# Stick-breaking attention: work by PSUM bank, suffix sums prepared on VectorE, values of two heads in turn, and the causal mask added by VectorE

## What is computed

```
z = einsum('bhqd,bhkd->bhqk', qb, kb) * scale
mask = s_pos < t_pos
log_keep = where(mask, log_sigmoid(-z), 0)
suffix = cumsum(log_keep, reverse) - log_keep
wts = where(mask, exp(log_sigmoid(z) + suffix), 0)
out = einsum('bhqk,bhkd->bhqd', wts, vb)
```

## Time and profile before

| | |
|---|---|
| median of 3 executions | 1835.47 us (1831.92 to 1836.16) |
| span of the profiled execution, first to last instruction | 1824.3 us |
| PE busy | 1705.0 us, 93% of the span |
| DVE, ACT busy | 647.0 us, 443.7 us |
| attention, first score to the end of the last values | 202.1 to 286.3 us, 84.2 us |

### The profile page before, as it was taken

The page is one execution under the profiler, slowest core; times in us unless marked ns, Lnnn a source line. Parts: engine busy times, 40 slices in busy tenths (PEclk is TensorE's granted clock), DMA queues, the critical chain, the costliest instruction groups (busy, mean ns, idle before and its releaser), DMA issues.

```text
span 1824.3 us, 21872 instructions
## 1 busy us (share of the span) xinstructions
PE 1705.0 (93%) x8774; PEld 885.3 (49%) x8774; DVE 647.0 (35%) x1210; ACT 443.7 (24%) x775; POOL 170.2 (9%) x172
## 2 busy tenths in 40 slices
PE   7999999889999999999699998999799999999983
PEld 3455564545445555455355548975433333333331
DVE  3379111242223122221269947542522221222213
ACT  2233552214312122111258512331100000000001
POOL 0000000011111111110000023100111111111110
PEclk9999999989999999999899999999799999999997
DMA  9274611389999999999480091044799999999994
GB/s 367 93 257 160 213 70 47 133 321 407 392 401 411 407 400 406 407 411 413 174 322 1 5 143 47 1 162 194 277 392 403 406 409 407 406 421 408 417 414 175
DMA packets 94220, 515.26 MB, mean 282 GB/s; under 512 B 22429, under 2 KB 28157, under 8 KB 69544
## 3 DMA queue, kind: packets, MB, share of 16 engines
q1 hardware_dynamic: 82920, 496.46, 70.0%
q0 software_dynamic: 11200, 17.39, 2.9%
HBM read 506.09 MB, written 27.05 MB: 292 GB/s over the span
## 4 chain that ended last, share of the span: by engine, by line
PE 70%; DMA 15%; issue 7%; DVE 5%; SPq 2%; ACT 1%; DVEq 0%; POOLq 0%
PE bank L852 22%; PE bank L868 10%; PE bank L454 8%; PE bank L462 8%; DMA ring<-in_w_up 7%; DMA ring<-in_w_down 4%; PE bank L809 3%; PE bank L839 3%; PE bank L730 2%; PE bank L879 2%; PE bank L520 2%; PE bank L685 2%; PE bank L447 1%; DVE arena L2549 1%; DMA ring<-diag 1%
## 5 line engine op out<-in xcount | busy, mean ns | idle before, releaser
L854 PE MATMUL bank<-ring,arena 128*64 128x512 f32 x928 | 418.7, 605 | 0.0
L852 PE MATMUL bank<-ring,arena 128*64 128x512 f32 x752 | 339.1, 604 | 9.4 <-DMA ring<-in_w_up 6.8
L868 PE MATMUL bank<-ring,arena 128*64 128x512 f32 x544 | 247.9, 598 | 2.6 <-DMA ring<-in_w_down 2.6
L870 PE MATMUL bank<-ring,arena 128*64 128x512 f32 x544 | 247.9, 598 | 0.0
L2448 DVE TENSOR_TENSOR arena<-arena,bank 64x512 f32<-64x512 f32 x70 | 48.3, 690 | 560.5 <-ACT arena L1763 560.5
L454 PE MATMUL bank<-arena,ring 128*128 128x512 f32 x560 | 244.6, 593 | 0.0
L852 PEld LDWEIGHTS bank<-ring,arena 128*64 128x64 f32 x752 | 100.7, 139 | 208.5 <-issue 202.4
L852 PE MATMUL bank<-arena 128*64 128x512 f32 x368 | 166.1, 605 | 9.3 <-DMA ring<-in_w_up 5.0
L1429 POOL DMA_INDIRECT arena<-xnd,smalli x70 | 67.6, 966 | 1074.4 <-PE bank L839 536.0
L454 PEld LDWEIGHTS bank<-arena,ring 128*128 128x128 f32 x560 | 105.2, 190 | 127.2 <-issue 127.2
L1763 ACT ACTIVATE arena<-bank 64x512 f32<-64x512 f32 x70 | 41.2, 588 | 512.1 <-PE bank L854 512.1
(11 more groups left out here) (439 smaller groups left out, 1999.2 us busy)
## 6 DMA issues: line engine op xcount, KB each, us to landing
ring<-in_w_down SPq DMA_DIRECT2D x62, 2048.0 KB, 33.2
ring<-in_w_up SPq DMA_DIRECT2D x54, 2048.0 KB, 16.9
ring<-in_w_gate SPq DMA_DIRECT2D x45, 2048.0 KB, 17.4
arena<-in_w_gate SPq DMA_DIRECT2D x19, 2048.0 KB, 25.2
ring<-in_w_mod SPq DMA_DIRECT2D x12, 2048.0 KB, 8.0
ring<-in_w_in SPq DMA_DIRECT2D x10, 2048.0 KB, 15.7
arena<-in_w_up SPq DMA_DIRECT2D x10, 2048.0 KB, 29.8
ring<-in_w_out SPq DMA_DIRECT2D x4, 2048.0 KB
```

The costliest lines, as they stand in the source:

```text
L852: pe.matmul(GU[0:CAP, :], x, wg_[:, c, :], start=(c == 0), stop=(c == KD - 1), skip_group_check=True)
L854: mm = pe.matmul(GU[CAP:2 * CAP, :], x, wu_[:, c, :], start=(c == 0), stop=(c == KD - 1), skip_group_check=True)
L868: pe.matmul(Y[0:CAP, :], x, wd_[:, c, 0:512], start=(c == 0), stop=(c == 3), skip_group_check=True)
L870: mm = pe.matmul(Y[CAP:2 * CAP, :], x, wd_[:, c, 512:1024], start=(c == 0), stop=(c == 3), skip_group_check=True)
```

## The change

Five edits, all in the attention:

1. By bank. `PIECES` orders a head's work: the third bank (256 columns), the second (chunks 1 and 3, 512 columns), the first (512 columns). `z_ready`, `ln_ready`, `sp_raw`, `arg_ready` and `w_raw` are counted three to a head, and each step waits only for its own bank. Exp and Ln of the softplus become three instructions each, interleaved.
2. Sums of later chunks. After two of its three instructions `scored` adds the columns of later chunks up on DVE into `below` (three additions of 128x128), and `decays` multiplies `nones` with these sums: nine products and 2048 columns in place of ten and 2560.
3. `values(p)` works on two heads: their products alternate between the lower and the upper 64 output partitions. It stands once for each pair, after `scores` of the pair's second successor.
4. Mask. The four identity products of `scores` go; a new `masked(h)` on DVE adds `far` to the four diagonal blocks in PSUM.
5. Order. PE runs `decays(2p)`, `scores(2p+2)`, `decays(2p+1)`, `scores(2p+3)`, `values(p)`; DVE runs `scored(h)`, `masked(h+1)`.

```diff
+        PIECES = ((2, 256, (2,)), (1, 512, (1, 3)), (0, 512, (0,)))
+        below = [area(5, 3072 + 384 * i, 384) for i in range(2)]
...
             def scores(h):
-                for c in (0, 1, 3, 2):
-                    pe.matmul(zpart(z, c), ...)
-                for c in range(4):
-                    mm = pe.matmul(zpart(z, c)[:, 0:P], M["ident"], far, start=False, stop=True,
-                                   skip_group_check=True)
+                for i, (bank, width, held) in enumerate(PIECES):
+                    if h >= 2:
+                        pe.wait_ge(S("w_raw"), 3 * (h - 2) + i + 1)
+                    for c in held:
+                        mm = pe.matmul(zpart(z, c), ...)
+                    mm.then_inc(S("z_ready"), 1)
...
             def decays(h):
-                for c in range(4):
-                    for c2 in range(c, 4):
-                        mm = pe.matmul(zpart(z, c)[:, P * (c2 - c):], M["nge"] if c2 == c else M["nones"],
-                                       kpart(spb[h % 2], c2), start=False, stop=(c2 == 3),
-                                       skip_group_check=True)
-                mm.then_inc(S("arg_ready"), 1)
+                pe.wait_ge(S("sp_raw"), 3 * h + 2)
+                less(2, 2, 4, M["nge"], kpart(sp, 2), False)
+                less(2, 3, 4, M["nones"], kpart(sp, 3), True).then_inc(S("arg_ready"), 1)
+                less(3, 3, 4, M["nge"], kpart(sp, 3), True)
+                less(1, 1, 4, M["nge"], kpart(sp, 1), False)
+                less(1, 2, 3, M["nones"], kpart(sp, 2)[:, 0:P], True)
+                pe.wait_ge(S("below"), 3 * h + 1)
+                less(1, 3, 4, M["nones"], bl[:, 2 * P:3 * P], True).then_inc(S("arg_ready"), 1)
+                pe.wait_ge(S("sp_raw"), 3 * h + 3)
+                less(0, 0, 4, M["nge"], kpart(sp, 0), False)
+                less(0, 1, 2, M["nones"], kpart(sp, 1)[:, 0:P], True)
+                pe.wait_ge(S("below"), 3 * h + 3)
+                less(0, 2, 4, M["nones"], bl[:, 0:2 * P], True).then_inc(S("arg_ready"), 1)
...
+            def values(p):
+                pe.wait_ge(S("w_raw"), 3 * (2 * p + 2))
                 for c in range(4):
+                    for i in range(2):
+                        h, r = 2 * p + i, HD * i
+                        mm = pe.matmul(o[r:r + HD, P * c:T], vtok[:, c, HD * h:HD * h + HD], kpart(wb[i], c),
+                                       start=(c == 0), stop=(c == 3), skip_group_check=True)
...
-            for h in range(NH):
-                decays(h)
-                if h:
-                    values(h - 1)
-                if h + 2 < NH:
-                    scores(h + 2)
-            values(NH - 1)
+            for p in range(NH // 2):
+                for h in (2 * p, 2 * p + 1):
+                    decays(h)
+                    if h + 2 < NH:
+                        scores(h + 2)
+                values(p)
...
             def softplus(h):
-                for b, w in ((0, 512), (1, 512), (2, 256)):
-                    last = A(lnb[:, 512 * b:512 * b + w], z[b][:, 0:w], ACT.Abs)
-                chain(last)
-                chain(A(lnb, lnb, ACT.Exp, scale=-1.0))
-                A(lnb, lnb, ACT.Ln, bias=one).then_inc(S("ln_ready"), 1)
+                absolute(0)
+                exponential(0)
+                absolute(1)
+                logarithm(0)
+                exponential(1)
+                absolute(2)
+                logarithm(1)
+                exponential(2)
+                logarithm(2)
...
+            def masked(h):
+                z = zbanks[h % 2]
+                for i, (bank, width, held) in enumerate(PIECES):
+                    dve.wait_ge(S("z_ready"), 3 * h + i + 1)
+                    for c in held:
+                        o = zpart(z, c)[:, 0:P]
+                        ins = TTo(o, o, far, ALU.add)
+                    ins.then_inc(S("z_masked"), 1)
...
             def scored(h):
+                    if i == 1:
+                        dve.wait_ge(S("sp_raw"), 3 * h + 2)
+                        TTo(bl[:, 2 * P:3 * P], kpart(sp, 2)[:, P:2 * P], kpart(sp, 3), ALU.add).then_inc(S("below"), 1)
+                        TTo(bl[:, 0:P], kpart(sp, 1)[:, P:2 * P], kpart(sp, 2)[:, 0:P], ALU.add).then_inc(S("below"), 1)
+                        dve.wait_ge(S("below"), 3 * h + 1)
+                        TTo(bl[:, P:2 * P], kpart(sp, 1)[:, 2 * P:3 * P], bl[:, 2 * P:3 * P], ALU.add)\
+                            .then_inc(S("below"), 1)
...
             for h in range(1, NH):
                 scored(h)
+                if h + 1 < NH:
+                    masked(h + 1)
```

More of the change, by code:

```diff
@@ L735, in values @@
[L735 to L741, removed]
+                for i, (bank, width, held) in enumerate(PIECES):
+                    if h >= 2:
+                        pe.wait_ge(S("w_raw"), 3 * (h - 2) + i + 1)
+                    for c in held:
+                        mm = pe.matmul(zpart(z, c), qk[r:r + HD, 4 + h // 2, P * c:P * c + P],
+                                       qk[r:r + HD, h // 2, P * c:T], start=(c != 3), stop=False,
+                                       skip_group_check=True)
+                    mm.then_inc(S("z_ready"), 1)
@@ new lines, in decays, with less @@
+            def decays(h):
+                z, sp, bl = zbanks[h % 2], spb[h % 2], below[h % 2]
+                def less(c, q0, q1, mat, src, last):
+                    return pe.matmul(zpart(z, c)[:, P * (q0 - c):P * (q1 - c)], mat, src, start=False, stop=last,
+                                     skip_group_check=True)
+                pe.wait_ge(S("sp_raw"), 3 * h + 2)
[11 more added lines that the diff above has]
+                less(0, 2, 4, M["nones"], bl[:, 0:2 * P], True).then_inc(S("arg_ready"), 1)
@@ L1308, in _ @@
             load_e(0, 3)
-            sp.wait_ge(S("z_ready"), NH)
+            sp.wait_ge(S("z_ready"), 3 * NH)
             sp.dma_start(x_tok, a["x"].rearrange("(t p) d -> p t d", p=P)).then_inc(S("x_again"), 16)
@@ L1698, in softplus, with part, marked, absolute @@
                 z = zbanks[h % 2]
-                act.wait_ge(S("z_ready"), h + 1)
-                if h:
-                    act.wait_ge(S("sp_raw"), 3 * h)
-                for b, w in ((0, 512), (1, 512), (2, 256)):
-                    last = A(lnb[:, 512 * b:512 * b + w], z[b][:, 0:w], ACT.Abs)
-                chain(last)
-                chain(A(lnb, lnb, ACT.Exp, scale=-1.0))
-                A(lnb, lnb, ACT.Ln, bias=one).then_inc(S("ln_ready"), 1)
+                def part(i):
+                    bank, width, _ = PIECES[i]
+                    return lnb[:, 512 * bank:512 * bank + width], z[bank][:, 0:width]
+                at = {}
+                def marked(ins, name):
+                    chained[0] += 1
+                    ins.then_inc(S("act_chain"), 1)
+                    at[name] = chained[0]
+                def absolute(i):
+                    act.wait_ge(S("z_masked"), 3 * h + i + 1)
+                    if h:
+                        act.wait_ge(S("sp_raw"), 3 * (h - 1) + i + 1)
+                    marked(A(part(i)[0], part(i)[1], ACT.Abs), f"abs{i}")
+                def exponential(i):
+                    act.wait_ge(S("act_chain"), at[f"abs{i}"])
+                    marked(A(part(i)[0], part(i)[0], ACT.Exp, scale=-1.0), f"exp{i}")
+                def logarithm(i):
+                    act.wait_ge(S("act_chain"), at[f"exp{i}"])
+                    A(part(i)[0], part(i)[0], ACT.Ln, bias=one).then_inc(S("ln_ready"), 1)
+                absolute(0)
[7 more added lines that the diff above has]
+                logarithm(2)
             def squared(p):
@@ L1718, in _ @@
                 z = zbanks[h % 2]
-                act.wait_ge(S("arg_ready"), h + 1)
                 if h >= 2:
-                    act.wait_ge(S("o_ready"), h - 1)
-                for b, w in ((0, 512), (1, 512), (2, 256)):
-                    A(wb[h % 2][:, 512 * b:512 * b + w], z[b][:, 0:w], ACT.Exp).then_inc(S("w_raw"), 1)
+                    act.wait_ge(S("o_ready"), h // 2)
+                for i, (bank, width, _) in enumerate(PIECES):
+                    act.wait_ge(S("arg_ready"), 3 * h + i + 1)
+                    A(wb[h % 2][:, 512 * bank:512 * bank + width], z[bank][:, 0:width], ACT.Exp).then_inc(S("w_raw"), 1)
                 if h + 2 < NH:
```

31 lines of the change are left out of this document (14 added, 17 removed).

## The result

The changed kernel takes 1809.38 us (median of 4 executions, 1806.15 to 1811.33), the kernel before 1835.37 beside it: a ratio of 0.9859, 95% interval 0.9844 to 0.9874.

The account below looks back on a forecast made before the run. PE was taken to set the attention's pace, and later stages to shift with it: 20.9 us saved less 2 for waits is 18.9, so 1835.5 - 18.9 = 1816.6, say 1817 us; range 1811 to 1825.5.

Parts of the forecast that it names:

- The work on PE: PE in the attention, a pair of heads: decays 7.0, scores 4.70, values 2.30, together 14.0 us, now 20.16.
- The walk: Attention followed joint by joint from the first score at 202.11: project at 265.4 before the allowance, 20.9 us sooner.
- The allowance: Semaphore waits within each engine's row, bounded by nothing and 4.0 us; half taken, 2 us, giving a gain of 18.9.
- The clock (D): Rival: PE's clock halves after the new 2.8 us stand at the start, losing 1.9 us; folded into the 62% forecast case.
- The loop (B): Rival: the loop through ACT and DVE is longer than summed; gain 11 to 16, 1820 to 1824.5 us; 22%.
- the values (C): Rival: values of two heads don't share the PE array, 4.6 us a pair; gain 9.7, 1826 us; 5%.
- slower (E): Rival: the loop takes 11.2 us, binding both heads of a pair; 7.4 us more than before, 1843; 4%.
- given back (F): Rival: the MoE waits for something not moving with PE, up to all lost; 1830 to 1841; 4% with smaller losses.
- The step that failed: From project to the end: each us by which project starts sooner is a us of the end; nothing else changes.
- The 11.2 us: Median's excess over the profiled span of 1824.3 us, taken as untouched by the change.
- or a better clock behind: Part of the more-than-forecast case, with a shorter start stand or a loop that never binds: down to 1811; 3%.

Follow-up runs that it names:

- the fourth profile: The changed kernel, unaltered, profiled a fourth time, with no slower rows behind its 2.14 us wait; execution 1807.97 us, attention 63.8 us.
- the first set: The first measurement of the changed kernel beside the kernel before: 1809.38 us against 1835.37, ratio 0.9859.
- the second set: The changed kernel, unaltered, measured again against the kernel before: 1810.43 us, ratio 0.9871 (0.9841 to 0.9901).
- weights within softplus: Changed kernel with the previous head's weights placed on ACT between the pieces of the next head's softplus: 1811.07 us, ratio 0.9880 to the kernel before.
- the kernel by bank: Changed kernel with identity products, all ten decays products and values head by head, leaving only work by bank and the new order: 1835.37 us, ratio 1.0008.

## Why the prediction was right in direction and wrong in size

**The work on PE.** Right: identity gone, values x16 in 2.30 to 2.37 us, scores as before. Decays are 3.68 in the chain for the 3.5 taken: 1.80 ns a column where the old ones had 1.70, with nine products for 2048 columns and not ten for 2560.

**The walk.** It holds within half a microsecond at every joint. Counted from the first score, in the fourth profile, which has no lowered clock: `decays(0)` at 6.6 (forecast 6.5), `scores(2)` at 12.5 (12.8), `decays(2)` at 23.6 (23.9), `decays(4)` at 38.3 (38.5), `project` at 63.8 (63.3). The wait at the start was 2.14 for 2.8, the loop's waits 0.23, 0.23 and 0.75 for 0.6 each, the end's 0.69 for 0.9.

**The allowance.** "I take half, 2 us" for waits on semaphores within ACT's rows. This term was mis-sized: the nine instructions of a softplus took 4.6 us with their waits, the masks 0.30 alone, and the walk without the allowance is what was measured.

**The clock (D).** It came, and bigger than its 1.9 us: up to 5.1. But "which before had not" holds for the length of the stand alone: the kernel before has a stand of 1.45 us and 0 to 3.3 us of slower rows behind it, which happened to be absent from the trace that was read. On the means of four profiles it costs 1.2 us before ((0 + 3.3 + 1.6 + 0) / 4) and 2.5 changed ((5.1 + 1.6 + 3.3 + 0) / 4), so it takes 1.3 from the gain. The allowance, 2 us too much, and the clock, left out at 1.3, nearly cancel: that the attention gained 19.4 where 18.9 were forecast is luck in part.

**The loop (B), the values (C), slower (E), given back (F).** B and E didn't happen; the waits stayed below the forecast. C is refuted by 2.37 against 3.93. (E's working has the end give back 4.5 us where its terms give 15.0 - 10.2 = 4.8; nothing hangs on it.) F is refuted for the first MoE: the stage ahead of it keeps its 85 us, and SP's next issue moved by the 16.2 us of `project`.

**The step that failed.** "So each us by which `project` starts sooner should be a us of the end", and of what lies beyond the span "nothing of it is touched": the sum put the change's gain outside the attention at nothing. `project` started 19.4 us sooner counted from the first score, on the mean of four profiles of each; the median fell by 26.0 in the first set and 23.4 in the second. Of the 7.1 us by which 26.0 exceeds the forecast, 0.5 come from the attention and 6.6 from outside it.

The 11.2 us were a misreading too. Only 1.9 lie around the span; the other 9 were an execution faster than the median, taken for a constant ("11.2 us of start and end around the first and last instruction", ahead of the prediction). The forecast is a difference from the median, so this moved it little (the kernel before, at 18 executions in the second set, has 1833.8, 1.7 lower than the 1835.5 started from). But it hid that outside the attention one execution differs from another by some 10 us. For that the range had "or a better clock behind", at 3% together with all else, down to 1811: 3.8 us for the waits and some 2 for the clock.

**The rest is open.** The second set's interval ((1 - 0.9901) and (1 - 0.9841) of 1833.8, 18 to 29 us) holds 19.4, the first set's ((1 - 0.9874) and (1 - 0.9844) of 1835.4, 23.1 to 28.6) doesn't. The 72 and 12 executions together differ by 23.8 us, by their spread 22.0 to 25.6, so chance is unlikely to be all of it. The profiles show 3.8 us behind the attention, of which 2.7 are not the clock, and 1.2 ahead, in stages with the same instructions. Over all seventeen profiles, the seven with identity products average 1539.1 us from `project` to the last output and the ten without 1536.0, with standard deviations of some 3. Without the time lost to the lower clock another grouping fits better: the six profiles of kernels that hand whole heads over have 1481.8 to 1483.7 there, ten of the eleven of kernels by bank 1478.8 to 1481.6, and one (weights within softplus) 1484.2. That hints at a link and doesn't show one, and no mechanism was found.

**What each edit is worth**, undone from the changed kernel, attention at the full clock: mask 10.5 (6.2 of it the alternation of tiles), paired values 6.1, sums 4.7, together 21.3. The three at once take the kernel by bank from 86.9 to 63.4, 23.5 us; undone one at a time they sum to less, since a part of what each saves PE then stands waiting. The order by bank by itself costs 2.7. With whole heads handed over the mask gives 3.3 us, 5.5 at the full clock, and the values cost time, 1.2 us at the full clock and 9.8 more at the lower one, since waits for ACT and DVE take the place of PE's work. The sums alone were not run on the kernel before.

## What to carry to other kernels

When PE sheds work in a loop with ACT and DVE, first shorten the hand-over between them (here a bank for a head), then take the work away: in the other order the same saving turned into waits, and one into a loss. Sort products by tile shape; alternating 64x128 with 128x128 cost 0.2 us a change here. And take more than one profile before the span of one becomes the base of a sum: here it was 8 to 9 us off the median.

## What the runs showed of the hardware

A wait of 1.45 us (with 0.64 before it) or of 2.14 us left PE at the lower clock in some executions of a kernel and not in others, and so did, in one profile each, one of 0.75 us (changed) and three of 0.73, 1.17 and 0.40 (weights within softplus). A place cost nothing, 1.6 to 1.8 us or 3.3 to 3.4. With three unused products in the wait the rows behind it were at full speed in the one profile taken; that the products did it is not shown. Over 72 executions of one program the time fell by some 1.4 us for each 0.001 of mean granted clock. Values of two heads behind each other take 3.93 us and not twice 2.30, alternating 2.37. Each change between tiles of 64x128 and 128x128 cost 0.2 us. ACT's instructions overlap by 0.1 us though each carries a wait that is already fulfilled: nine in 4.6 us, where they add up to 5.05 alone. DVE adds 128x128 in place in PSUM in 0.30 us, four behind each other in 0.88.
